# One step of a hybrid mixer and mixture-of-experts network: second layer's modulation products moved into the first layer's merge, cumulative sums, rotary and convolution taps rearranged

## The reference

```python
mod = (silu(cond) @ w_mod + b_mod)          # 6 x 1024 per layer, for two conditions
sh1, sc1, g1, sh2, sc2, g2 = split(mod, 6)
h = rms(x, norm1) * (1 + sc1) + sh1
proj = h @ w_in                             # all mixers' inputs and the gates
y_m = mlstm(fwd) + mlstm(bwd)               # chunked, log forget gates summed along time
y_d = diff_attention(rope(q), rope(k), v)   # rotary for latent tokens only
la  = log_sigmoid(g_a @ w_up + b) / 16      # GLA decay per key channel
y_g = gla(q, k, v, cumsum(la))              # forward and backward
y_c = silu(layernorm(conv31(c_a * sigmoid(c_b))))    # depthwise, 31 taps
out = sum_n sigmoid(gate_n) * (y_n @ w_branch_n) @ w_out
x = x + g1 * out
h = rms(x, norm2) * (1 + sc2) + sh2
x = x + g2 * experts(h)                     # best group, two of its four experts
```

## Time and profile before

| What | Value |
|---|---|
| Median of three runs | 2091.97 us |
| Profiled execution, its own time | 2090.02 us |
| Its span, first to last instruction | 2088.0 us |
| TensorE / VectorE / ScalarE / GpSimd busy | 1994.8 / 725.4 / 476.5 / 86.8 us |
| Mean granted TensorE clock | 0.982 |
| DMA, mean rate over the span | 200 GB/s |

### The profile page before, as it was taken

One profiled execution on the slowest core, in us unless ns is written; L12 is line 12 of the kernel. 1 busy time (PEld: TensorE's weight loads), 2 busy tenths in 40 slices (PEclk: granted clock), 3 DMA queues, 4 the chain that ended last, 5 costly groups with the idle time before them and its releaser, 6 DMA issues.

```text
span 2088.0 us, 29588 instructions
## 1 busy us (share of the span) xinstructions
PE 1994.8 (96%) x12618; PEld 1088.3 (52%) x12618; DVE 725.4 (35%) x1927; ACT 476.5 (23%) x932; POOL 86.8 (4%) x119
## 2 busy tenths in 40 slices
PE   6989999999999979999989999999999997999997
PEld 3444556656655544444445565665665554444443
DVE  1292666333311131222223966632331113122223
ACT  2311234344200121111133133324420012111112
POOL 0000100000000010000020010000000001000002
PEclk9999999999999989999989999999999998999998
DMA  9777661221222548999952223121213243799993
GB/s 395 252 275 280 219 245 45 89 97 70 74 108 101 201 157 330 395 391 393 391 191 112 81 88 125 45 80 66 111 61 121 101 200 149 285 392 394 389 406 138
DMA packets 44403, 419.74 MB, mean 201 GB/s; under 512 B 5632, under 2 KB 5776, under 8 KB 18160
## 3 DMA queue, kind: packets, MB, share of 16 engines
q1 hardware_dynamic: 30240, 369.56, 45.6%
q0 software_dynamic: 7312, 24.68, 3.3%
q10 hardware_dynamic: 6720, 23.60, 3.2%
HBM read 389.21 MB, written 28.61 MB: 200 GB/s over the span
## 4 chain that ended last, share of the span: by engine, by line
PE 87%; DMA 6%; another core or an unknown queue 3%; ACT 1%; DVE 1%; issue 1%; POOL 1%; SPq 0%; POOLq 0%; ACTq 0%; DVEq 0%
PE psum L742 16%; PE psum L1023 16%; PE psum L1128 9%; PE psum L1038 8%; PE psum L1149 6%; PE psum L745 6%; PE psum L1133 5%; PE psum L1070 4%; DMA pc<-we_in 2%; PE psum L660 2%; PE psum L850 2%; DMA ring<-wch_in 1%; DMA ring<-wmod_in 1%; DMA ring<-we_in 1%; PE psum L720 1%
## 5 line engine op out<-in xcount | busy, mean ns | idle before, releaser
L742 PE MATMUL psum<-hT,ring 128*128 128x384 f32 x1088 | 366.6, 490 | 2.0 <-ACT pc L1307 1.9
L1023 PE MATMUL psum<-hT,ring 128*128 128x384 f32 x1024 | 343.2, 488 | 0.0
L742 PEld LDWEIGHTS psum<-hT,ring 128*128 128x128 f32 x1088 | 202.3, 190 | 142.6 <-issue 16.3
L1023 PEld LDWEIGHTS psum<-hT,ring 128*128 128x128 f32 x1024 | 192.1, 190 | 130.6
L1038 PE MATMUL psum<-pc,ring 128*128 128x384 f32 x512 | 175.6, 486 | 0.0
L1753 DVE SCALAR_TENSOR_TENSOR pc<-pc,par 128x128 f32<-128x128 f32 x480 | 159.4, 415 | 0.0
L2189 DVE TENSOR_TENSOR ytok<-pc,psum 128x384 f32<-128x384 f32 x32 | 17.7, 554 | 353.0 <-ACT pc L1580 353.0
L2145 DVE COPY scr<-psum 64x512 f32<-64x512 f32 (+1 forms) x180 | 91.8, 510 | 114.8 <-PE psum L1149 113.2
L1128 PE MATMUL psum<-ring,scr 128*64 128x512 f32 x512 | 117.7, 613 | 12.1 <-issue 10.0
L1038 PEld LDWEIGHTS psum<-pc,ring 128*128 128x128 f32 x512 | 95.5, 190 | 61.5
L745 PE MATMUL psum<-ring,hT 128*128 128x512 f32 x288 | 126.5, 594 | 0.0
(11 more groups left out here) (349 smaller groups left out, 2073.2 us busy)
## 6 DMA issues: line engine op xcount, KB each, us to landing
ring<-we_in SPq DMA_DIRECT2D x48, 2048.0 KB, 17.8
pc<-we_in SPq DMA_DIRECT2D x48, 2048.0 KB, 18.5
ring<-wmod_in SPq DMA_DIRECT2D x42, 1024.0 KB, 6.1
ring<-wch_in SPq DMA_DIRECT2D x18, 2048.0 KB, 9.0
ring<-wgate_in SPq DMA_DIRECT2D x16, 2048.0 KB, 7.8
ring<-wbr_in SPq DMA_DIRECT2D x16, 1024.0 KB, 7.9
ring<-wtok_in SPq DMA_DIRECT2D x6, 2048.0 KB, 7.6
expert_out_rows<-scr ACTq DMA_DIRECT2D x30, 384.0 KB, 9.4
```

The lines of the kernel that those rows point to most:

```text
L742: mm = pe.matmul(F[:, 0:T], wv[:, k, n * P:(n + 1) * P], hT[:, k, :], start=k == 0, stop=k == KD - 1)
L1023: mm = pe.matmul(bank(5 + n % 2)[:, 0:T], wv[:, k, (n % 4) * P:(n % 4 + 1) * P], hT[:, k, :], start=k == 0, stop=k == KD - 1)
```

## The change

Seven edits come together.

1. The 24 halves of the second layer's modulation leave the units. The 14 halves of layer 0 that are left follow units 2 to 15, one each. The 24 others stand between `gate` and `branch` of steps 14 to 31 of layer 0's merge, one, one, two and so on. ScalarE loads them, each in two DMAs (768 KB and 256 KB), into three buffers (slots `GQK`, `CA`, `DKK` of `pc`, and a part of `vals`); the load of half n + 3 is issued after the gate of the step behind half n's step is opened. Turning and adding them moves into the output projection.
2. The GLA gate products put channels on the partitions at once (four products of 384 columns instead of three of 512). The cumulative sums are eight scans on VectorE, without the division by 16, which goes into the scale of the exponentials. The sixteen triangular products and four copies are gone.
3. A tap is one instruction per channel group, over three pieces of 128 tokens that are each padded by themselves. All 31 taps come before the mLSTM loop.
4. The rotary partner rows are fetched by DMA from GpSimd's queue (four per block of 32 rows), and VectorE rotates all four heads at once, for queries and for keys.
5. The GLA outputs are issued as twelve 128-row products, eight 64-row products alternating between the heads, four 128-row products (counted as instructions in the profile).
6. The scores of both components of one step are issued in alternation.
7. With the swap products gone, the wait for the gated GLA outputs moves behind the last unit. `swap` and `tri_b` leave the constants.

```diff
 def halves_after(u):
-    todo = 2 * (DEPTH * NMOD - HEAD)
-    return range(2 * HEAD + min(todo, u * 3 // 2), 2 * HEAD + min(todo, (u + 1) * 3 // 2))
+    todo = 2 * (NMOD - HEAD)
+    return range(2 * HEAD + min(todo, u), 2 * HEAD + min(todo, u + 1))
+LATE_FIRST, LATE_PAIRS = 14, 18
+def late_halves(m):
+    count, n = 2 * (DEPTH - 1) * NMOD, m - LATE_FIRST
+    return range(2 * NMOD + count * n // LATE_PAIRS, 2 * NMOD + count * (n + 1) // LATE_PAIRS)
...
+        late_w = [(pc_flat[:, s * 4 * T:(s + 1) * 4 * T], vals[:, 3 * W + i * W:3 * W + (i + 1) * W])
+                  for i, s in enumerate((GQK, CA, DKK))]
...
# TensorE: GLA gates
-                        for t in range(NT):
-                            mm = pe.matmul(bank(t), gaT[0:64, tok(t)], w_up, start=True, stop=True)
+                            mm = pe.matmul(bank(v)[:, 0:T], w_up[:, lc], gaT[0:64, :], start=True, stop=True)
...
-                            pe.matmul(B[:, CTX], la[:, 0, lc], tri[d], start=True, stop=True)
...
# TensorE: GLA outputs
                         for t in range(NT):
                             pe.matmul(bank(4 + hh)[:, tok(t)], g_att[d][:, hh * 3 + t, :], gv[:, t, head * P:(head + 1) * P],
                                       start=(d == 0 and t == 0), stop=False, skip_group_check=True)
-                        for t in (1, 2):
+                    for t in (1, 2):
+                        for hh in range(2):
+                            r = slice(64 * hh, 64 * hh + 64)
                             pe.matmul(bank(4 + hh)[:, tok(t)], g_qs[d][r, tok(t - 1)], S0[r, d, pair, :],
                                       start=False, stop=False, skip_group_check=True)
...
# TensorE: before the scores
-                rotate_two(4)
-                unit(U_DIFF + 5, lambda: rotate_two(6))
+                unit(U_DIFF + 5)
                 unit(U_DIFF + 6)
-                pe.wait_ge(rot_used.sem, rot_used.at(l, 8))
+                pe.wait_ge(fin_done.sem, fin_done.at(l, 2))
+                pe.wait_ge(rotated_s.sem, rotated_s.at(l, 2))
...
# TensorE: merge
+                if l == 0:
+                    pe.wait_ge(dpv_copied.sem, dpv_copied.at(l, 12))
                 for m in range(14, 32):
                     gate(m)
+                    if l == 0:
+                        for half in late_halves(m):
+                            mod_half(half)
                     branch(m)
...
# ScalarE
+                def load_late(n):
+                    m, half = divmod(2 * NMOD + n, 2)
+                    src = wmod_d[bass.ds(m, 1)].rearrange("a p n -> (a p) n")
+                    of = half * HALF
+                    ac.dma_start(late_w[n % 3][0], src[:, of:of + 3 * W]).then_inc(mod_in[n % 3].sem, 16)
+                    ac.dma_start(late_w[n % 3][1], src[:, of + 3 * W:of + 4 * W]).then_inc(mod_in[n % 3].sem, 16)
...
                 for m in range(14, 32):
                     gate_open(m)
+                    if l == 0 and m > LATE_FIRST:
+                        for half in late_halves(m - 1):
+                            if half + 3 < 2 * DEPTH * NMOD:
+                                ac.wait_ge(mod_done.sem, half + 1)
+                                load_late(half + 3 - 2 * NMOD)
+                if l == 0:
+                    mod_copy(2)
...
# VectorE: cumulative sums and taps
+                for v in range(4):
+                    for a, b in ((0, SEQ), (SEQ, T)):
+                        s = slice(a, b) if v % 2 == 0 else slice(b - 1, a - 1 if a else None, -1)
+                        o = ve.tensor_tensor_scan(gT[:, v, s], ones[:, 0:1].to_broadcast([P, b - a]), la[:, v, s], 0.0,
+                                                  ALU.mult, ALU.add)
+                    o.then_inc(g_ready.sem, 1)
...
+                for j in range(CW):
+                    for c in range(4):
+                        src = upad[:, c, :, j:j + P]
+                        dst = pc[:, CA, c, :].rearrange("p (t n) -> p t n", t=NT)
...
+                        chain.settle(but=3)
+                        o = ve.scalar_tensor_tensor(dst, src, taps[:, c, j:j + 1], dst, ALU.mult, ALU.add)
...
# VectorE: rotary, once per block
+                    ve.wait_ge(partner_in[i].sem, partner_in[i].at(l, 64))
+                    ve.tensor_tensor(other, other, over_heads("sin"), ALU.mult).then_inc(partner_x.sem, 1)
+                    step(ve.tensor_tensor(v, v, over_heads("cos"), ALU.mult))
...
# GpSimd
+                def fetch_partners(i):
+                    slot = (DQ, DKK)[i]
+                    gp.wait_ge(unit_copied.sem, unit_copied.at(l, units_to("ch", slot)))
+                    for q in range(4):
+                        to, of = slice(32 * q, 32 * q + 32), slice(32 * (q ^ 1), 32 * (q ^ 1) + 32)
+                        gp.dma_start(partner[i][to], pc[of, slot, :, LAT]).then_inc(partner_in[i].sem, 16)
```

More of the change, by code:

```diff
@@ L294, in hybrid_step @@
                 [zB[:, lv, :] if lv < 4 else zC[:, lv - 4, :] for lv in range(7)]]
+        partner = [pc_flat[:, MQ * 4 * T + i * H * DEC:MQ * 4 * T + (i + 1) * H * DEC].rearrange("p (h t) -> p h t", h=H)
+                   for i in range(2)]
         g_ca = pc_flat[:, MQ * 4 * T + LEVELS * T:MQ * 4 * T + LEVELS * T + 2 * P]
@@ L343, in hybrid_step @@
         slot_in = [sig(f"slot{i}_in", 0) for i in range(6)]
-        mod_in = [sig(f"mod_half{i}_in", 0) for i in range(2)]
+        mod_in = [sig(f"mod_half{i}_in", 0) for i in range(3)]
         mod_done = sig("mod_half_done", 0)
@@ L387, in hybrid_step @@
         fin_done = sig("fin_done", 3)
-        rot_done = sig("rot_done", 8)
-        rot_used = sig("rot_used", 8)
+        partner_in = [sig(f"partner_rows{i}_in", 64) for i in range(2)]
+        partner_x = sig("partner_rows_scaled", 2)
+        rotated_s = sig("rotated", 2)
         sc_done = sig("sc_done", 24)
@@ L1332, in _ @@
                         ac.wait_ge(la_done.sem, la_done.at(l, 1))
-                        for t in range(NT):
-                            chain.step(ac.activation(scrB[:, t * 512:(t + 1) * 512], bank(t), ACT.Abs))
+                        for v in range(4):
+                            chain.step(ac.activation(gT[:, v, :], bank(v)[:, 0:T], ACT.Abs))
                         chain.settle()
@@ L1727, in _ @@
                 ve.wait_ge(la_exp.sem, la_exp.at(l, 1))
-                for t in range(NT):
-                    o = ve.scalar_tensor_tensor(la[:, t, :], bank(t), 0.0, scrB[:, t * 512:(t + 1) * 512],
-                                                ALU.min, ALU.subtract)
+                for v in range(4):
+                    o = ve.scalar_tensor_tensor(la[:, v, :], bank(v)[:, 0:T], 0.0, gT[:, v, :], ALU.min, ALU.subtract)
+                    if v < 3:
+                        step(o)
                 o.then_inc(la_ready.sem, 1)
+                ve.wait_ge(la_ready.sem, la_ready.at(l, 1))
@@ L1733, in _ @@
+                chain.settle()
+                for v in range(4):
+                    for a, b in ((0, SEQ), (SEQ, T)):
[3 more added lines that the diff above has]
+                    o.then_inc(g_ready.sem, 1)
                 ve.wait_ge(cb_sig.sem, cb_sig.at(l, 1))
@@ L1759, in _ @@
-                conv_taps(range(CONV_FIRST))
+                for j in range(CW):
+                    for c in range(4):
+                        src = upad[:, c, :, j:j + P]
+                        dst = pc[:, CA, c, :].rearrange("p (t n) -> p t n", t=NT)
+                        if j == 0:
+                            step(ve.tensor_scalar(dst, src, taps[:, c, 0:1], None, ALU.mult))
+                            continue
+                        chain.settle(but=3)
+                        o = ve.scalar_tensor_tensor(dst, src, taps[:, c, j:j + 1], dst, ALU.mult, ALU.add)
+                        if j == CW - 1 and c == 3:
+                            o.then_inc(conv_v.sem, 1)
+                        else:
+                            step(o)
@@ L1933, in _ @@
                 o.then_inc(fin_done.sem, 1)
-                for n in range(4, 8):
-                    rotated(n)
+                rotated(1)
                 def d_weights(v):
@@ L2018, in _ @@
                     o.then_inc(out_used.sem, 1)
+                    if l == 0 and n == 3:
+                        add_mod(2)
                 ve.wait_ge(out_used.sem, out_used.at(l, 8))
@@ L2326, in _constants @@
     put("ident", s == t)
-    put("swap", (s // 64 == t // 64) & (s % 32 == t % 32) & (s != t))
     n_freq = DQK // 4
@@ L2335, in _constants @@
     put("tri_f", (s <= t) / 16.0)
-    put("tri_b", (s >= t) / 16.0)
     put("sixteenth", np.full((P, P), 1 / 16.0))
```

191 lines of the change are left out of this document (79 added, 112 removed).

## The result

The changed kernel takes 2081.76 us (median of five runs, 2078.68 to 2082.71) beside 2094.81 us for the kernel before in five runs: a ratio of 0.9938, 95% interval 0.9926 to 0.995. That is 13 us faster where 25 were forecast, and outside the range of 2056 to 2080. The profiled execution took 2080.67 us for a span of 2078.9, 9.1 us under the span before. Twelve to sixteen of the forecast's microseconds are missing; the profile has to say where.

The account below looks back on a forecast made before the run. TensorE, busy 1994.8 of 2088.0 us, was taken as the bound. Gains of 31.3 us less 6.0 lost made net 25 us, giving 2066 us, with a range of 2056 to 2080.

Parts of the forecast that it names:

- step 6: Layer 0's merge: late loads mostly hidden, four waits beside 2 MB fills, 3 us lost together, lower bound 0, upper 28 us.
- rival (a): Layer 0's merge: late loads really late, stalls bringing half speed, kernel slower, 2104 us at mean landing 11.5; chance 0.05.
- The 8 us that the prediction made of the rule: Layer 0's merge: if DMA engines alternate queues by packets of 9 to 17 descriptors, four waits total some 8 us, not 3.
- The row of 11.0 us: Earlier profile: 384 KB expert load on ScalarE's queue beside busy SP queue took 11.0 us; used for the 28 us upper bound.
- rival (b): Layer 0's merge: late loads partly late, mean landing near 9.5 to 10 us, kernel 2078 us; chance 0.12.
- Waits and half speed in the first projections: Layer 0's first projections: 7.9 us of modulation-weight waits and 2.45 us from half clock speed both go.
- The halves: Layer 0: 14 single halves cost 16.7 us, 24 in the merge 26.7; 43.4 against 41.4 before, 2.0 us lost.
- Cumulative sums: GLA gates, both layers: sixteen TensorE products per layer go, 3.57 us each, 7.1 in all; VectorE scans hidden.
- GLA outputs: GLA stage: reordered products of two heads overlap, 0.86 us gained in each of eight passes, 6.9 us; 3.4 without overlap.
- Rotary: Before the scores, both layers: sixteen swap products per layer leave TensorE, 3.4 us each, 6.9 over both.
- The wait for copied columns: Before layer 0's mLSTM loop: a half that covered part of this wait leaves, making it about 1.0 us longer.
- Covers: Taps hidden before the mLSTM loop with 2.4 us to spare in layer 1; rotary key rows with 3 us; price 0.

Follow-up runs that it names:

- kernel without bytes: Changed kernel with weight fills of layer 0's steps 16 to 31 and first half of output weights cut to 64 columns per partition; 3388 us, merge stretch 295.3 us.
- old order: Changed kernel with late halves loaded earlier, but GLA outputs issued head by head as in the kernel before; 2066.17 us, ratio 0.9882.
- move alone: Kernel before with only the second layer's modulation halves moved into layer 0's merge, loaded early; 2081.15 us, ratio 0.9948.
- after: The changed kernel with all its edits, against the kernel before; 2081.76 us, ratio 0.9938.
- early: Changed kernel, but ScalarE issues each late half's load before opening the next step's gate; 2061.59 us, ratio 0.9862 to the kernel before.
- yield: Changed kernel, but SyncE holds the four 2 MB fills of the late stretch until the late half has landed; 2065.31 us, ratio 0.9883.
- both of shorter rows: Changed kernel with layer 0's 2 MB merge fills split into four DMAs (4 KB rows; 2060.53 us) or two (8 KB rows; 2065.63 us).
- threes: Changed kernel with early loads, but the 24 late halves in eight groups of three at steps 16, 18, ... 30; 2056.22 us, ratio 0.9821.
- the kernel without the move: Changed kernel with modulation left as in the kernel before, 38 halves after layer 0's units and none in the merge; 2065.08 us, ratio 0.9882.

## Why the prediction was wrong

**The term that failed** is step 6: "I take four waits, 3 us together", from "a late load issued with it needs up to some 10 to 11". The four places were right. The landings were 12.9 to 13.2 and 10.9 us, the waits 13.4 us, and the half speed that three of them brought, which the prediction named in rival (a) but put into no term of the forecast, 8.6 more: 22 us in place of 3. The working took 7.9 us for a branch half behind a fill and added a little. In that row the second transfer stood in the same queue, behind the fill, with rows of 8 KB; on another queue it shares row by row, and a half with rows of 6 and 2 KB gets the small part. Each of the 16 DMA engines has 8 such rows of each kind, so the half is through only after 16 rows of SyncE's: 8 x 16 + 8 x 8 KB on each engine, all 3 MB. The engines moved 401 GB/s from 534 to 540 us, and a fill of 32 KB in the kernel without bytes landed after 2.4 us: as an estimate from these two, 4.2 MB make 12.9 us. The same count gives 10.3 and 7.6 for rows of 8 and 4 KB, measured 10.4 and 8.3, and 10.3 where no branch fill follows, measured 10.9.

The Trainium skill (DMA: Bandwidth & Descriptors, Queues, rings and completion order) has the engines go round the queues by packets. The trace agrees that they take turns, 128 against 121 packets in 8.3 us, but what it shows as a packet is a single row, not 9 to 17 descriptors, and 36 rows of the half had moved when 44 of the fill's 128 had: the measurement decides. The 8 us that the prediction made of the rule were too few as well. The row of 11.0 us, put aside because "SP's queue is empty for three quarters of the merge", was the nearest one: the load is issued by the same event as the fill, so what counts is not how often the queue is empty but that it never is at these four moments.

What came about is nearest to rival (b), landings late in part, at a larger price: four late by much, not a mean of 9.5 to 10 (the page's median landing is 6.8 us). Rival (a)'s condition, nearly every half late, did not come about.

**The other steps**, each from the traces:

- Waits and half speed in the first projections, 7.9 + 2.45: both gone; the first mLSTM product stands at 175.98 (near 175).
- The halves: 26.6 us in the merge (26.7), 17.3 more than layer 1 for 14 single ones (16.7).
- Cumulative sums: layer 1 up to the mLSTM loop 103.9 to 100.4, 3.5 us (3.57).
- GLA outputs: 6.7 by the old order (6.9).
- Rotary: not run by itself. From the end of the mLSTM stage to the first score, layer 0 gained 6.3 us and layer 1 5.9, where GLA outputs and rotary together were to give 6.9 each.
- The wait for copied columns ahead of layer 0's mLSTM loop: 0.54 to 1.54 us, the 1.0 as said.
- Covers: they held, not all by the margins given. VectorE's timeline in layer 1, and TensorE's first mLSTM product:

```profile
1127.70 1.88 DVE L1746 TENSOR_TENSOR_SCAN scr<-cst,scr 128x128 f32<-128x128 f32 x4
...
1144.62 63.59 DVE L1770 SCALAR_TENSOR_TENSOR pc<-pc,par 128x384 f32<-128x384 f32 x120
1208.62 0.69 DVE L1781 SCALAR_TENSOR_TENSOR vals<-psum,vals 128x512 f32<-128x512 f32 x1 [0.41 <-POOL vals L2264]
```

```profile
1210.46 0.83 PE L813 MATMUL psum<-mva,vals 128*128 128x129 f32 x6
```

  Layer 1 begins 2.2 us later in this trace. Less that, the mLSTM product stands at 1208.3 as worked out, and the taps, 0.530 us each (0.527), end at 1206.0 instead of 1205.0. With the two operations that TensorE needs (till 1209.5) 1.0 us of room is left, not 2.4. A scan over 128 partitions costs what one over 4 does (1.88 us for four; 2.02 in the earlier trace rows). The partner rows of layer 0's keys landed 8.7 us after the last issue and were rotated by 377, 6.0 us ahead of the first score.

Layer 1 gained 11.9 us from first unit to first score against 10.5: the 2.2 us in which TensorE waited for its own instructions ahead of the GLA stage (1296.12 before) are gone. No edit touches that place; layer 0 still shows 1.76 us there (at 259.68), the kernel with the move alone 1.9 us in layer 1. Why is open. From layer 0's output projection to layer 1's first unit, the seven kernels that do not differ in it (after, early, yield, both of shorter rows, old order, threes) took 403.1 to 408.2 us. A difference of 5 us between two profiled spans can come from there alone, and so stages had to be compared instead.

## What to carry to other kernels

Before adding a load to a second queue, see what event issues it: if the same event issues a large fill on another queue, the two collide each time, and an average load of the queue says nothing. Then count rows, not bytes: here the small transfer was through after as many rows of the other queue as it has itself, so give the urgent one long rows or the patient one short ones, or issue it a step earlier. A stall of 3 us on TensorE should be priced with the half speed that can come with it, which here added two thirds of the wait again.

## Not expected of the hardware

- Two hardware queues on the same DMA engines alternated row by row: 16 KB rows and 6 KB rows in equal number, so that the one got 2.05 and the other 0.73 MB in 8.3 us.
- Fills in rows of 4 KB instead of 16 KB brought no wait for gate weights, though issuing the four parts took 2.2 us of SyncE's queue.
- Waits of 3.60 to 4.77 us in the merge came with 6.8 us at 1.2 GHz, waits of 2.14 and 3.00 with 3.4 us, waits up to 1.42 with none; but a wait of 3.62 us in the first projections (the kernel without the move) came with none either. What decides this is open.
